# Two weight pieces of one expert, loaded as sixteen transfers of eight rows each

## The reference

```python
def moe_swiglu(h, router_w, w1, w3, w2):
    logits = (h @ router_w).astype(jnp.float32)
    top_v, top_i = lax.top_k(logits, TOP_K)
    top_p = jax.nn.softmax(top_v, axis=-1)
    gates = ...
    y = jnp.zeros_like(h)
    for e in range(N_EXPERTS):
        y = y + gates[..., e:e + 1] * swiglu(h, w1[e], w3[e], w2[e])
    return y
```

## Time and profile before

| | |
|---|---|
| median of 3 runs | 1246.83 us |
| lowest and highest | 1246.26, 1246.98 us |
| the profiled execution's own time | 1244.92 us |
| span of the profile | 1243.1 us |
| mean granted clock of PE | 0.993 |
| PE busy | 1187.7 us (96%) |
| DMA packets, all queues | 60863, 460.12 MB |

### The profile page before, as it was taken

The page is one execution under the profiler, slowest core; times in us unless marked ns, Lnnn a source line. Parts: engine busy times, 40 slices in busy tenths (PEclk is TensorE's granted clock), DMA queues, the critical chain, the costliest instruction groups (busy, mean ns, idle before and its releaser), DMA issues.

```text
span 1243.1 us, 33898 instructions
## 1 busy us (share of the span) xinstructions
PE 1187.7 (96%) x15397; PEld 763.8 (61%) x15397; DVE 429.3 (35%) x853; ACT 222.8 (18%) x375; POOL 16.8 (1%) x34
## 2 busy tenths in 40 slices
PE   8999999999999999998999987999999999999876
PEld 6757999999997654554654443555455545554433
DVE  4588799999776001120110120120102001100203
ACT  4375533333443000000000000000000000000002
POOL 0500000000000000000000000000000000000000
PEclk9999999999999999999999999999999999999999
DMA  9962798988845999999999999999999999999993
GB/s 391 382 234 101 283 392 348 365 332 340 312 170 217 391 399 406 413 419 421 418 419 420 420 419 420 420 417 420 419 420 419 420 419 419 420 419 419 419 404 119
DMA packets 60863, 460.12 MB, mean 370 GB/s; under 512 B 6960, under 2 KB 7344, under 8 KB 9392
## 3 DMA queue, kind: packets, MB, share of 16 engines
q1 hardware_dynamic: 59376, 455.78, 89.9%
q10 hardware_dynamic: 1344, 2.16, 0.5%
HBM read 456.81 MB, written 1.11 MB: 368 GB/s over the span
## 4 chain that ended last, share of the span: by engine, by line
PE 64%; DVE 14%; DMA 10%; SPq 7%; issue 3%; ACT 1%; DVEq 0%; ACTq 0%
PE bank L2305 34%; PE bank L2319 15%; DMA ring<-in_moe 9%; SPq L601 7%; DVE work L1122 6%; DVE split L1106 4%; PE bank L1847 4%; DMA ring<-in_mixa 2%; PE bank L1919 1%; PE bank L2287 1%; PE bank L1739 1%; PE bank L2277 1%; DVE ring L1396 1%; DVE split L1407 1%; PE bank L2055 1%
## 5 line engine op out<-in xcount | busy, mean ns | idle before, releaser
L2305 PE MATMUL bank<-ring,work 128*32 128x256 f32 x9408 | 523.5, 382 | 29.1 <-DMA ring<-in_moe 16.1
L2305 PEld LDWEIGHTS bank<-ring,work 128*32 128x32 f32 x9408 | 315.0, 111 | 242.7 <-issue 59.5
L2319 PE MATMUL bank<-ring,moe 128*32 128x512 f32 x2352 | 261.5, 593 | 7.4 <-DMA ring<-in_moe 7.4
L1671 DVE TENSOR_TENSOR moe<-moe,bank 128x256 f32<-128x256 f32 (+1 forms) x84 | 28.2, 384 | 611.8 <-ACT moe L1009 611.8
L2319 PEld LDWEIGHTS bank<-ring,moe 128*32 128x32 f32 x2352 | 76.0, 110 | 173.8 <-issue 144.3
L1009 ACT ACTIVATE moe<-bank 128x256 f32<-128x256 f32 (+1 forms) x84 | 24.4, 357 | 742.1 <-PE bank L2305 742.1
L2140 PE MATMUL bank<-split 128*128 128x256 f32 x1024 | 125.4, 283 | 0.8 <-DVE split L1106 0.7
L2140 PEld LDWEIGHTS bank<-split 128*128 128x128 f32 x1024 | 123.7, 192 | 1.6 <-DVE split L1106 1.2
L1106 DVE TENSOR_TENSOR split<-ring,split 128x2048 fp32r<-128x2048 f32 x33 | 75.5, 2289 | 7.4 <-ACT split L902 3.3
L1122 DVE SCALAR_TENSOR_TENSOR work<-ring,condp,work 128x512 f32<-128x512 f32 x98 | 73.6, 751 | 4.2
L902 ACT ACTIVATE split<-ring 128x2048 fp32r<-128x2048 f32 x31 | 59.3, 1914 | 75.0 <-PE bank L2140 72.7
(11 more groups left out here) (277 smaller groups left out, 613.6 us busy)
## 6 DMA issues: line engine op xcount, KB each, us to landing
ring<-in_moe SPq DMA_DIRECT2D x336, 1024.0 KB, 26.6
ring<-in_ffn SPq DMA_DIRECT2D x16, 2048.0 KB, 8.7
ring<-in_ada SPq DMA_DIRECT2D x28, 1024.0 KB, 7.4
ring<-in_ada SPq DMA_DIRECT2D x10, 2048.0 KB, 9.6
ring<-in_mixout SPq DMA_DIRECT2D x2, 2048.0 KB, 8.3
ring<-in_fnet SPq DMA_DIRECT2D x2, 2048.0 KB, 8.8
ring<-in_mixa SPq DMA_DIRECT2D x2, 1024.0 KB, 15.0
tail<-tables ACTq DMA_DIRECT2D x8, 256.0 KB, 8.4
```

Of the source, the lines that this page charges most:

```text
L1671: nc.vector.tensor_tensor(gate_e[:, g, 0:n], gate_e[:, g, 0:n], bank[g][:, n:2 * n], ALU.mult).then_inc(e_hidden, counts_for(light, g))
L2305: last = mm(out[:, :, block, :], x_group[:, 4 * half + k, j * CAP + g * QUAD:j * CAP + (g + 1) * QUAD], source[:, :, k, :, c, :], start=(h ...
L2319: last = mm(bank[3 + n][c * QUAD:(c + 1) * QUAD, :], hiddenT[phase % 2][:, g, blk * QUAD:(blk + 1) * QUAD], source[:, j, n * 512:(n + 1) * ...
```

## The change

The pieces at queue places 18 and 19 of the fourth expert (place 3, in group 0), which are the first two of the four of its down phase 0, are no longer loaded by one DMA of 128 rows each. `load_by_eights` issues sixteen DMAs of eight rows (64 KB) for each. The last one of a piece raises the slot's semaphore, as before; the other fifteen raise a shared one, `eighths_in`, which is `half_in[0]` used again. PE waits in this one down phase for the 30 parts of both pieces on `eighths_in` before its first matmul, and then for each slot's semaphore as before. All other loads and all the arithmetic are the same.

```diff
--- before.py
+++ after.py
@@ -113,6 +113,7 @@
 GROUP_PIECES = GROUP * PIECES
 FIRST_GROUP = GROUP_PIECES - 2
 SLOTS = 16
+BY_EIGHTS = (3, (18, 19))
 QUEUE_AT = {("up", 0, 0): 0, ("up", 0, 1): 4, ("down", 3): 8, ("up", 1, 0): 10, ("up", 1, 1): 14, ("down", 0): 18,
             ("up", 2, 0): 22, ("up", 2, 1): 26, ("down", 1): 30, ("up", 3, 0): 34, ("up", 3, 1): 36, ("down", 2): 38}
 
@@ -392,6 +393,7 @@
         part_ready, part_added = ([sem(f"{name}{pair}") for pair in range(4)] for name in ("part_ready", "part_added"))
         ada_done = sem("ada_done")
         half_in, half_free = [sem(f"half_in{n}") for n in range(HALF_BUFFERS)], [sem(f"half_free{n}") for n in range(HALF_BUFFERS)]
+        eighths_in, eighths_before = half_in[0], 16 * len(range(0, HALVES, HALF_BUFFERS))
         sum_ready, scaled_summed = sem("sum_ready"), sem("scaled_summed")
         dve_step, pool_step = sem("dve_step"), sem("pool_step")
         out_ready, stored = sem("out_ready"), sem("stored")
@@ -599,6 +601,12 @@
             def load(slot, e, q):
 
                 sp.dma_start(landed(slot), moe_d[e, q]).then_inc(piece_in[slot], 16)
+
+            def load_by_eights(slot, e, q):
+
+                for lo in range(0, P, 8):
+                    part = sp.dma_start(landed(slot)[lo:lo + 8, :], moe_d[e, q][lo:lo + 8, :])
+                    part.then_inc(piece_in[slot] if lo + 8 == P else eighths_in, 16)
 
             def first_load(n):
 
@@ -651,7 +659,10 @@
                         sp.wait_ge(e_used, PIECES * i - 2)
                     elif q % 2 == 0:
                         sp.wait_ge(e_used, PIECES * i + (q - SLOTS))
-                    load(slot_of_piece(group, j, q), before if AHEAD <= q < AHEAD + 2 else e, q)
+                    if isinstance(i, int) and i == BY_EIGHTS[0] and q in BY_EIGHTS[1]:
+                        load_by_eights(slot_of_piece(group, j, q), e, q)
+                    else:
+                        load(slot_of_piece(group, j, q), before if AHEAD <= q < AHEAD + 2 else e, q)
 
             for n in THEN:
                 first_load(n)
@@ -2308,9 +2319,11 @@
                                           start=(half == 0 and block == 0 and k == 0), stop=(half == 1 and k == 3), skip_group_check=True)
                     last.then_inc(e_used, 2)
 
-            def down(phase, turned, light, slots, counts):
+            def down(phase, turned, light, slots, counts, eighths=0):
 
                 pe.wait_ge(e_turned, turned)
+                if eighths:
+                    pe.wait_ge(eighths_in, eighths_before + 16 * 15 * eighths)
                 for at, (slot, count) in enumerate(zip(slots, counts)):
                     pe.wait_ge(piece_in[slot], 16 * count)
                     source = landed(slot).rearrange("p (j n) -> p j n", j=2)
@@ -2326,7 +2339,8 @@
             def down_of(i, phase, turned, light, group, j):
 
                 qs = [QUEUE_AT["down", phase] + at for at in range(2 if phase == 3 else 4)]
-                down(phase, turned, light, [slot_of_piece(group, j, q) for q in qs], [landings(group, j, q) for q in qs])
+                down(phase, turned, light, [slot_of_piece(group, j, q) for q in qs], [landings(group, j, q) for q in qs],
+                     len([q for q in BY_EIGHTS[1] if q in qs]) if isinstance(group, int) and i == BY_EIGHTS[0] else 0)
 
             def turn_tables():
```

## The result

The changed kernel takes 1260.68 us (median of 4 runs, 1258.5 to 1261.69) against 1246.57 us for the kernel before (median of 4, 1246.26 to 1246.98). The ratio is 1.011, 95% interval 1.0098 to 1.0122: slower by 14.1 us, where 4.8 us less had been forecast.

A forecast was written before the change was run, and what follows sets the result against it. The prediction took the weight stream, ended by its late DMA engines, as the bound. From the 1246.83 us median, -4.8 us for shifted load, with issue and wait costing nothing, gave 1242.0 us; own range 1241.0 to 1244.2, 8-in-10 range 1241.0 to 1252.2.

The forecast's parts named there:

- What bounds the kernel: From 500 us the weight stream never pauses and sets the end; only time saved for the last DMA engine counts.
- Bytes per engine: For the two pieces, eight engines carry +5.0 us, the others -5.0; with the early ones loaded, a gain of 4.4 to 5.0.
- the term of -4.8 us: At the stream's end, the gain taken from loading the early eight engines, chance 0.50 with the gain kept.
- Issue: SP issues 30 more DMAs, 10 to 23 us, covered by the queue's backlog of some 27 us; costed at 0.
- Wait: In the fourth expert's down phase PE starts 1.8 to 2.5 us later, absorbed by its waits in the eighth expert.
- Narrow writes: Eight-row transfers of the two pieces may slow the stream, up to 8 to 9 us scaled by bytes; taken as 0 to 1.
- the drag eats the gain: Rival: narrow writes slow all engines; 1246.8 us at half price (0.17 with even dealing), 1250.5 at the whole (0.10).
- The late eight get the load: Rival: at the stream's end the loaded engines are the late ones, +5.0 us, 1251.8 us; chance 0.13.
- Eight rows can be written only so fast: Rival: a port rate limits each eight-row transfer to 1.25 us, 40 us for 32; 1272.4 us, chance 0.10.
- The signs: 224 more short packets, little or no 222 GB/s plateau, last landing near 1221, PE's filled stretch 1 to 2.5 us later.

The follow-up runs named there:

- e12: The change made at the third expert instead of the fourth; 1259.04 us against 1246.39 for the kernel before.
- e5: Against the kernel before, both pieces as eight transfers each of all 128 rows and 256 columns; 1247.57 us against 1246.73.
- e6: Against the kernel before, both pieces without rows 64 to 127, rows 0 to 63 in eight transfers of eight rows four apart; 1244.45 us against 1246.73.
- e11: Against the kernel before, one piece without rows 64 to 127, its rows 0 to 63 loaded twice, eight rows four apart; 1246.64 us against 1246.39.
- e1: The changed kernel with the eight rows of each transfer four apart instead of neighbours; 1255.49 us against 1246.24 for the kernel before.
- e4: Against the kernel before, both pieces as eight transfers each of sixteen rows, eight apart; 1256.47 us against 1246.24.
- e2: Against the kernel before, both pieces as eight transfers each of sixteen neighbouring rows; 1258.46 us against 1246.24.
- e8: Against the kernel before, both pieces as two transfers each of 64 rows; 1254.83 us against 1246.73.
- e7: As e6, without rows 64 to 127, but each transfer has eight neighbouring rows; 1251.84 us against 1246.73 for the kernel before.
- e9: As e6, writing rows four apart, but reading eight neighbouring rows of memory; 1245.06 us against 1246.39 for the kernel before.
- e10: As e7, writing eight neighbouring rows, but reading rows of memory four apart; 1252.58 us against 1246.39 for the kernel before.

## Why the prediction was wrong, step by step

*What bounds the kernel*: held. The time that the stream lost in one stretch is the greater part of the loss of the kernel, 11.6 of 14.1 us at the fourth expert and 9.5 of 12.6 at the third (e12). Lost time at a share below 1, which early engines can absorb, did not count (e5). That is the distinction "for the DMA engine that is last" that the prediction made.

*Bytes per engine*: half right. 224 more short packets is what eight engines for each transfer give. The Trainium skill's rule on the number of engines (page "DMA: Bandwidth & Descriptors", section "Why a DMA increments its semaphore by 16 and not by 1") agrees with that count. That they are the same eight each time is borne out by the tails of the changed kernel, e6 and e11. But I asked only whether the loaded eight were the early or the late ones. By the tails, with two packets in flight in the changed kernel, e11 and e12, they are neither: two of the late engines are among them, and the other six loaded ones are early. So the last engine is not relieved by shifting load to the loaded eight, and the gain of 4.4 to 5.0 us could not come at all. e11, the shift without the drag, shows +0.3 us where it should have shown a gain of up to 2.5. So the term of -4.8 us failed as well. The prediction's own row had said only "about half"; that the two halves must be the same two halves was my addition. The cause that I gave for the lateness, the instruction fetches, was not tested. It fits better than my 15 us for each engine: only 82 of the 122 fetches come after 500 us, 87 us of packet time, 10.9 us for each of eight engines, against a measured difference of 9.4.

*Issue*: held in the changed kernel. An issue takes 0.28 us at the median, 9 us for 32; with the longer ones, up to 4.6 us, they went out over 22 us (first start 703.2, last 725.1), under the backlog of 26 to 32 us. The share stays at 1.01. It was close: in e1, at 0.64 us each, the cover ran out and the share fell to 0.55.

*Wait*: small by itself. e5 waits for all parts too, and its whole cost is 0.8 us (at most 2.2 by the interval). The phase started 16.7 us late, not 1.8 to 2.5, and that is the drag.

*Narrow writes*: this is the step that failed. I took 0 to 1 us of a range up to 9, and it was 11.6 us. I had the row for it: the earlier trace rows, 315 GB/s at a share of 1.08, is the same picture, all engines busy and slow, in the kernel before. By the list, 32-row transfers are mostly out of place as well, if the engines take the rows in order; that this dip has the same cause was not tested. I put it aside because its rows were of 2 KB and because engines that run apart rarely meet. The first was no reason: rows of 8 KB have the drag. For the second there is no evidence: two or four engines on a group cost about the same (e4, e2), and e8 has it with transfers of 512 KB. Scaled by bytes the dip gave 8 to 9 us, which would have been the better price by far.

*The rivals*: "the drag eats the gain" was the right one and held too narrow, since it kept the gain: 1250.5 at its worst, measured 1260.7. Without the gain its scaled price gives 1246.8 + 8.5 = 1255.3. "The late eight get the load" (1251.8) is true of two engines of the eight. "Eight rows can be written only so fast" overrated it (1272.4), and its mechanism does not fit: e4 writes no neighbouring rows and loses as much as e2.

*The signs*: the 224 short packets came. The others did not: a plateau and a long tail remained, the last landing was at 1240.9, and PE's last wait before its filled stretch ends at 807.4 us in place of 791.0, not 1 to 2.5 us later but 16.4. The sign for the drag had the wrong place. It asked for less than 400 GB/s right after 704 us, but the rate is 418 until 725, as what is issued at 704 lands some 27 us later.

Of the 14.1 us, 11.6 are time of the stream lost in the slow stretch. The remaining 2.5 fit the two late engines that carried the doubled load, whose tail is seen, but 1260.68 against e2's 1258.46 has overlapping intervals and e11 gave less than expected. How it divides is left open. Also open is the mechanism inside the chip by which one engine's misplaced rows slow all sixteen; the packet records do not name the engine.

## What to carry to other kernels

Where whole 128-row transfers stream at the full rate, a cut by rows that gives engines other rows than their own can nearly halve the rate of everything in flight beside it; it did so here with 8, 16 and 64 rows (239 GB/s from 725 to 752 us at the worst). If a piece has to be cut, cut it by columns (+0.8 us). Rows four apart that stay with their engine cost nothing, but that was tried only on the first 64 rows (e6). A dip in GB/s at a full DMA share was the mark of it here, and wherever one is already in the profile of before, it is the price to use. Before load is shifted between engines, find out engine by engine which are late; a plateau that says "half of them" does not say that it is the half that can be addressed.

## What the runs showed of the hardware that I had not expected

- A transfer's rows decide its cost by which engine writes them: 419 GB/s against 325 for the same bytes, engines and count (e6, e7), and it is the writing side (e9, e10).
- The slowdown hits all sixteen engines at once, with a share of 1.01 at 239 GB/s and 99% of the 8 KB packets slow, and costs more per byte for one piece (6.6 us of the stream) than for two (11.6 us).
- Two transfers of 64 rows in place of one of 128, for two pieces of 1 MB, cost 8.1 us.
- SP issues an eight-row transfer of neighbouring rows in 0.28 us, one of rows four apart in 0.64 us, a whole one in 0.33 us.
- Eight engines are late at the end, which the instruction fetches fit as the cause, and two of these are among the eight that an eight-row transfer uses (two packets in flight from 1234 to 1239 us).
